# A mixture-of-experts block on one core: the gate and up matrices of the ring are loaded in two halves of 2 MB instead of one piece of 4 MB

## The reference, cut to what matters

```python
g = xb @ w_gate_e[e] + b_gate_e[e]
u = xb @ w_up_e[e] + b_up_e[e]
g = jnp.minimum(g, SWIGLU_LIMIT)
u = jnp.clip(u, -SWIGLU_LIMIT, SWIGLU_LIMIT)
act = (u + 1.0) * (g * jax.nn.sigmoid(SWIGLU_ALPHA * g))
return act @ w_down_e[e] + b_down_e[e]
```

## Time and profile before

| | |
|---|---|
| median of 3 runs | 1227.37 us (1227.33 to 1227.81) |
| the profiled execution: its own time | 1229.45 us |
| the profiled execution: span of the profile | 1227.7 us |
| TensorE matrix products, busy | 1167.4 us, 95% of the span |
| VectorE, ScalarE, GpSimd, busy | 24%, 14%, 3% |
| moved by the DMA queue of SP | 452.47 MB in 49934 packets, 89.2% of the 16 engines' span |

### The profile page before, as it was taken

How to read it: one execution, slowest core, us unless ns; L and a number is a source line. 1 busy time by engine, 2 the same in 40 slices (tenths; PEclk the granted TensorE clock), 3 DMA queues, 4 the chain that set the end, 5 groups by cost and what they waited for, 6 DMA issues and landing times.

```text
span 1227.7 us, 13693 instructions
## 1 busy us (share of the span) xinstructions
PE 1167.4 (95%) x5597; PEld 581.7 (47%) x5598; DVE 294.5 (24%) x611; ACT 177.4 (14%) x354; POOL 41.3 (3%) x35
## 2 busy tenths in 40 slices
PE   9999999999999999989999989898988989898996
PEld 7588888885533434333343424333333333342432
DVE  2915656212322120211112120202021111111112
ACT  3123433102210101101010001000010101010102
POOL 1000005500000000000000000000000000000000
PEclk9999999999999999999999999999999999999999
DMA  9655534685899999999999999999999999999996
GB/s 275 199 177 206 205 138 159 252 312 219 308 427 428 428 432 430 431 427 433 429 433 429 432 429 435 425 437 425 438 428 432 429 430 432 429 431 426 435 423 263
DMA packets 49962, 452.86 MB, mean 369 GB/s; under 512 B 7284, under 2 KB 8430, under 8 KB 30734
## 3 DMA queue, kind: packets, MB, share of 16 engines
q1 hardware_dynamic: 49934, 452.47, 89.2%
HBM read 450.35 MB, written 1.06 MB: 368 GB/s over the span
## 4 chain that ended last, share of the span: by engine, by line
PE 66%; DMA 31%; DVE 1%; SPq 1%; issue 0%; ACT 0%; DVEq 0%; ACTq 0%
PE bank L1612 25%; PE bank L1350 17%; DMA arena<-in_w_up_e 16%; PE banks L1612 9%; DMA arena<-in_w_gate_e 8%; DMA w_gate_sb<-in_w_gate_e 5%; PE banks L1561 3%; DMA w_down_sb<-in_w_down_e 3%; PE bank L1509 2%; PE bank L1367 1%; PE banks L1384 1%; PE bank L1384 1%; PE bank L1648 1%; PE banks L1744 1%; PE banks L1800 1%; PE bank L1800 1%
## 5 line engine op out<-in xcount | busy, mean ns | idle before, releaser
L1612 PE MATMUL bank<-arena 128*64 128x512 f32 x1024 | 237.2, 609 | 22.8 <-DMA arena<-in_w_gate_e 14.8
L1350 PE MATMUL bank<-arena,w_down_sb 128*128 128x256 f32 x960 | 210.0, 380 | 0.0
L1350 PEld LDWEIGHTS bank<-arena,w_down_sb 128*128 128x128 f32 x960 | 181.3, 190 | 26.8 <-issue 1.5
L1612 PEld LDWEIGHTS bank<-arena 128*64 128x64 f32 x1024 | 71.9, 139 | 163.1 <-issue 147.3
L1612 PE MATMUL bank<-w_gate_sb,arena 128*64 128x512 f32 x512 | 120.0, 617 | 9.7 <-DMA w_gate_sb<-in_w_gate_e 9.6
L1612 PE MATMUL bank<-w_up_sb,arena 128*64 128x512 f32 x512 | 113.3, 594 | 13.8 <-DMA w_up_sb<-in_w_up_e 13.8
L1612 PE MATMUL bank<-w_down_sb,arena 128*64 128x512 f32 x480 | 105.5, 592 | 0.0
L1225 DVE TENSOR_SCALAR arena<-bank 128x512 f32<-128x512 f32 x32 | 22.1, 692 | 258.3 <-PE bank L1612 257.0
L1612 PEld LDWEIGHTS bank<-w_up_sb,arena 128*64 128x64 f32 x512 | 35.8, 137 | 86.1 <-issue 65.5
L1612 PEld LDWEIGHTS bank<-w_gate_sb,arena 128*64 128x64 f32 x512 | 35.9, 140 | 82.0 <-issue 67.3
L1137 DVE TENSOR_TENSOR arena<-banks,g2T 128x512 f32<-128x512 f32 (+1 forms) x32 | 21.9, 684 | 202.2 <-PE banks L1561 201.4
(11 more groups left out here) (318 smaller groups left out, 832.2 us busy)
## 6 DMA issues: line engine op xcount, KB each, us to landing
w_down_sb<-in_w_down_e SPq DMA_DIRECT2D x30, 2048.0 KB, 34.5
arena<-in_w_up_e SPq DMA_DIRECT2D x13, 4096.0 KB, 39.5
w_up_sb<-in_w_up_e SPq DMA_DIRECT2D x13, 4096.0 KB, 37.6
arena<-in_w_gate_e SPq DMA_DIRECT2D x13, 4096.0 KB, 30.8
w_gate_sb<-in_w_gate_e SPq DMA_DIRECT2D x12, 4096.0 KB, 30.2
arena<-in_w_down_e SPq DMA_DIRECT2D x14, 2048.0 KB, 29.3
w_gate_sb<-in_w_down_e SPq DMA_DIRECT2D x14, 2048.0 KB, 29.3
w_down_sb<-in_w_in SPq DMA_DIRECT2D x12, 2048.0 KB, 8.1
```

What stands on the lines that cost most here:

```text
L1350: ins = eng.matmul(ps[:, n * T:(n + 1) * T], w[:, k, (2 * b + n) * P:(2 * b + n + 1) * P], rhs[:, k, :], start=(k == 0), stop=(k == KC - 1))
L1612: ins = eng.matmul(ps[b * JB:(b + 1) * JB, :], lhsT, w[:, h * CH:(h + 1) * CH], **flags)
```

## The change

All gate and up matrices of the ring are loaded with `expert_load`, half by half. Each half has its own wait for its place and raises its own semaphore. `whole_load` and the constant `HALVES` go.

```diff
-            def whole_load(m, slot, expert):
-
-                src = A[m][0][expert, :, :].rearrange("a (p k) n -> p (a k) n", p=P)
-                eng.dma_start(ring[slot][:, :, :], src).then_inc(half_loaded[slot][0], 16)
-                eng.sem_inc(half_loaded[slot][1], 16)
-
...
-            def load(it, i, x, expert, whole=False):
-
-                if whole:
-                    place_free(it, i, x, 1)
-                    whole_load(MATRICES[x], pair_slot(i, x), expert)
-                    return
+            def load(it, i, x, expert):
+
                 for q in range(NQ):
                     place_free(it, i, x, q)
                     expert_load(MATRICES[x], pair_slot(i, x), q, expert)
...
-                load(0, i, x, slice(expert, expert + 1), x < 4 and m >= 6 * HALVES + 3)
+                load(0, i, x, slice(expert, expert + 1))
...
-                        load(n, i, x, expert_of(at + job_of(x)), x < 4)
+                        load(n, i, x, expert_of(at + job_of(x)))
...
-            load(more, AHEAD, 0, first, True)
-            load(more, AHEAD, 1, first, True)
+            load(more, AHEAD, 0, first)
+            load(more, AHEAD, 1, first)
             load(more, AHEAD, 2, second)
             load(more, AHEAD, 3, second)
```

More of the change, by code:

```diff
@@ L43 @@
 RING = 5
-HALVES = 2
 WARM = 10
```

## The result

The changed kernel takes 1231.3 us (median of 7 runs, 1230.44 to 1232.09) against 1227.37 us of the kernel before (7 runs). The ratio of the runs is 1.0027, with a 95% interval of 1.0018 to 1.0036; that is 3.3 us, from 2.2 to 4.4; the two medians are 3.9 us apart. The forecast was 3.4 us. The profiled execution took 1230.61 us, with a span of 1228.9. Here and in the experiments the ratios and their intervals leave out slow runs, over 1.5% above the fastest of their kernel: one of e5 (1493.3 us, granted clock 0.76) and four of the six of e2.

A forecast was written before the change was run, and what follows sets the result against it. One unbroken stream of transfers, full since about 337 us, plus a 20 us tail was taken to bound the kernel. 51 matrices at 0.067 us add 3.4 us: 1227.37 + 3.4 = 1230.8 us, range 1228.5 to 1233.5.

The forecast's parts named there:

- The stream sets the end: Whole ring: one unbroken stream of transfers, full since about 337 us, fixes the end; TensorE's earlier start does not.
- the same 20 us: Kernel's end: tail after the last down matrix lands, 1227.7 - 1207.66 = 20 us, only shifted by the change.
- Rival B: Loop: TensorE starts 4.9 us sooner and its pace sets the loop's; up to 70 us saved, 1157 us; chance 0.05.
- 5.5 us at most: Last pair: the most TensorE's earlier start could save there alone, giving 1222 us.
- 0.067 us a matrix: Loop's queue: extra cost of a gate or up matrix in two halves over a whole; times 51, 3.4 us.
- The check by quarters: Last down matrices: quarters against halves cost 11 ns a packet, which would make the sum 4.5 us.
- the 8 ns from wholes and halves: Full queue: from wholes to halves, 8 more packets per engine cost 0.067 us a matrix, 8 ns a packet.
- Rival A: Loop: halves as cheap as wholes or nearly, at or under 4.887 us each; 1227.4 to 1229.8 us; chance 0.27.
- Rival C: Loop: with only halves queued, they cost more than the samples, 6.3 us in all, 1233.7 us; chance 0.12.
- The 4.924: Ring's start, 350.86 to 395.18 us: nine earliest halves, 4.924 us each, giving the high sum of 6.3 us.
- Rival D: SP's queue in the loop: nine or ten transfers whatever their size, issues held up to 4.9 us; real cost chance 0.01.
- a constant 2.1 us: Whole kernel: median of the runs 2.1 us below the profiled execution, taken over to the forecast: 1230.8 against 1232.9 us.

The follow-up runs named there:

- e5: Changed kernel, TensorE waiting for both halves of a gate or up matrix before using the first, from pair 1 on except the last pair; 1231.04 us, ratio 1.0035.
- e2: Kernel before, each of 51 whole loads cut by partitions into two transfers of 64 partitions, packets still 32 KB; 1767.65 to 1902.95 us, ratio 1.449.
- e4: Changed kernel, TensorE waiting for both halves of a gate or up matrix before using the first, from pair 1 on, last pair included; 1234.4 us, ratio 1.0054.
- e6: Kernel before, with the gate and up matrix of the last pair's second job loaded whole too, 53 wholes instead of 51; 1230.51 us, ratio 1.0023.
- e8: Kernel before, unchanged, run once more for a second profiled execution; 1229.47 us.
- e7: Kernel before, with 26 down matrices loaded whole as well, TensorE taking gate and up columns in alternating groups of 4; 1225.84 us, ratio 0.9987.
- e1: Kernel before, each of 51 whole loads still one transfer but taken as two 16 KB runs a partition, so 16 KB packets; 1231.23 us, ratio 1.0028.
- e3: Changed kernel, every 2 MB half of the ring from matrix 6 on taken as two 8 KB runs a partition; 1244.57 us, ratio 1.0138.

## Why the prediction was right

**The stream sets the end.** Shown. The end moved with the landing of the last down matrix and the same 20 us lay behind it; the periods are those of the queue; e5 took TensorE's earlier start away and lost nothing. Rival B falls: where the DMA share is 1.00, TensorE gained nothing by starting sooner. In the last pair it can: e4 and e6 lost 3 us there by making TensorE late. The prediction put it at 5.5 us at most and did not see that the kernel before already had it: the second job of its last pair came in halves before the change too.

**The size.** 0.067 us a matrix was forecast and (58.73 - 58.44) / 4 = 0.073 was measured; 51 times that is 3.7 us. From the first landing of the ring to the last down matrix the traces give 3.0 us (against the kernel before) and 3.6 (against e8), and the runs 3.3 (2.2 to 4.4). That a forecast from landings given to 0.1 us came within a few tenths is in part luck: by the prediction's own account 0.025 us of error in a half, times 102, is 2.5 us. The check by quarters, 11 ns a packet, was a little high, and the 8 ns from wholes and halves a little low. The experiments give the law. For each DMA engine a pair has 48 packets in e7, 64 before, 96 after and in e1, 192 in e3:

| kernel | packets a pair and engine | transfers a pair | period, us | by 57.82 + 0.0095 x packets |
|---|---|---|---|---|
| e7 | 48 | 6 | 58.28 | 58.28 |
| before | 64 | 8 | 58.44 | 58.43 |
| e1 | 96 | 8 | 58.75 | 58.73 |
| after | 96 | 12 | 58.73 | 58.73 |
| e3 | 192 | 12 | 59.65 | 59.64 |

The two constants are fitted to these periods: 9.5 ns a packet, from 8 KB to 32 KB, and nothing for a transfer that 0.02 us a pair could show. Without packets, 25.17 MB in 57.82 us would be 435 GB/s, an estimate that reaches beyond the measured cases. The Trainium skill's page "DMA: Bandwidth & Descriptors", section "Where 436 GB/s comes from", puts the ceiling of the 16 ports at 435.2 GB/s; this case's intercept agrees. The same section lets a limit of about 358 GB/s bind between HBM and SBUF; this one core moves 428 to 431, and the measurement decides. The 2.0 us fixed for a transfer of the same page's "Anatomy of one DMA", a section on transfers that GpSimd issues, does not appear in this full queue of SP: e1 and the changed kernel differ by four transfers a pair and by 0.02 us.

**Rival A** falls, since the spacing in the loop is 4.894 and not at or under 4.887. **Rival C** falls: with nothing but halves in the queue they cost no more. The 4.924 was the mean of nine halves, and the trace of the kernel before shows what raised it: seven of them land 4.89 to 4.90 us behind the one ahead, the other two, at 365.66 and 395.19, 4.98 and 5.05 behind. What held up these two was not tried. **Rival D**: SP was not held in the loop of the changed kernel, whose longest issue between 540 and 1120 us takes 0.361 us; this step failed, as nine halves stay within the limit. e3 shows that the limit is not one of transfers, and that being held does not cost the stream anything, as the prediction had it.

**What failed beside it.** The forecast took the profiled execution and the runs to differ by a constant 2.1 us. They do not: the profiled execution is 2.1 us above the median in the kernel before, where TensorE's clock fell at 316 us, and 0.7 below it in the changed one, where it did not. So the profiled execution came in 2.3 us below the 1232.9 forecast for it. The forecast of the median was not touched, since it added the price to the median of the runs. Had I gone by the spans, 1.2 us, I would have called the result a third of what it is.

## What to carry to other kernels

When one queue is full without a gap, read prices from the distances between landings; how early a transfer is issued or its first half used is worth nothing until the last transfers. In such a queue the longest run of bytes for each partition wins, by 9.5 ns for each packet saved. A transfer of 128 partitions cut into two that keep the length of the runs and all 128 partitions cost nothing here (e1 against the changed kernel); cut by partitions, it made the kernel 45% slower (e2). Where work of another engine must fit between the last landings, at the end, the finer split earns its packets many times over: 2.8 us against some 0.15 for two matrices in e6.

## What the runs showed of the hardware that I had not expected

A stream whose gate and up matrices come in transfers of 64 partitions moves 244 GB/s with all 16 DMA engines busy, against 430 with 128 partitions in every transfer (e2). TensorE's granted clock can differ between executions at the same place of the same TensorE program: 0.64 and 0.74 in the two of the kernel before, 1.00 in the changed kernel and in e6, from 316 to 320 us. Where it was lower, the ring began 1.4 to 2.4 us later.
